# Passes in place of products: the order of the split matmuls within a weight panel, and the halves of a low part at layer doors

## What is computed

```python
# first block (also for a context of 256 tokens, up to w_in)
h = h + 0.5 * g * ((silu(n1(h) @ wg) * (n1(h) @ wu)) @ wd)       # 1024 -> 2816 -> 1024
p = n2(h) @ w_in                                                 # 1024 -> 6144
y = sigmoid(ga) * (o_a @ w_pa) + sigmoid(gb) * (o_b @ w_pb)      # recurrence and long convolution
h = h + m5 * (y @ w_out)
h = h + 0.5 * g * ((silu(n3(h) @ wg) * (n3(h) @ wu)) @ wd)
h = rms_norm(h) * final_norm_w
# second block, twice
proj = rms_norm(h) @ w_in                                        # 1024 -> 7424
h = h + sum(sigmoid(gates) * (branch @ w_branch)) @ w_out        # attention, retention, attention
h = h + relu(rms_norm(h) @ w_mlp_in)**2 @ w_mlp_out              # 1024 -> 4096 -> 1024
```

## Time and profile before

| | us |
|---|---|
| median of 3 runs | 1932.89 |
| lowest, highest | 1930.70, 1933.24 |
| the profiled execution, its own time | 1930.86 |
| its span, first to last instruction | 1929.1 |
| PE busy | 1869.6 (97%) |
| DVE busy | 1269.8 (66%) |
| POOL busy | 590.2 (31%) |
| ACT busy | 356.8 (18%) |

### The profile page before, as it was taken

How to read it: one execution, slowest core, us unless ns; L and a number is a source line. 1 busy time by engine, 2 the same in 40 slices (tenths; PEclk the granted TensorE clock), 3 DMA queues, 4 the chain that set the end, 5 groups by cost and what they waited for, 6 DMA issues and landing times.

```text
span 1929.1 us, 32922 instructions
## 1 busy us (share of the span) xinstructions
PE 1869.6 (97%) x13570; PEld 1712.2 (89%) x13570; DVE 1269.8 (66%) x1424; ACT 356.8 (18%) x655; POOL 590.2 (31%) x745
## 2 busy tenths in 40 slices
PE   4999999998999999999999999999999999999999
PEld 2777777887989979999999998999999999999999
DVE  6663222436268987666687976876667897687666
ACT  3100000103121221211132123321112212432110
POOL 1111111111236313333333222343434332244333
PEclk8999999999999999999999999999999999999999
DMA  9335665331333425354544333444554433344452
GB/s 367 118 109 217 252 245 216 129 109 44 110 132 117 157 88 181 148 179 177 193 154 153 134 131 129 153 175 176 188 181 175 153 132 131 120 162 172 180 180 104
DMA packets 44912, 307.35 MB, mean 159 GB/s; under 512 B 5376, under 2 KB 5888, under 8 KB 8320
## 3 DMA queue, kind: packets, MB, share of 16 engines
q1 hardware_dynamic: 40912, 292.66, 41.4%
q10 hardware_dynamic: 3888, 13.03, 1.9%
HBM read 302.53 MB, written 3.15 MB: 158 GB/s over the span
## 4 chain that ended last, share of the span: by engine, by line
PE 88%; DVE 7%; DMA 1%; issue 1%; ACT 1%; POOL 1%; SPq 0%; DVEq 0%; ACTq 0%; POOLq 0%
PE ps L1898 26%; PE ps L1899 25%; PE ps L1900 25%; PE ps L2030 2%; DMA landing<-in_stream 1%; DVE wlo L681 1%; DVE wlo L683 1%; PE ps L2397 1%; DVE xlo L745 1%; PE ps L2421 1%; PE ps L2407 1%; PE ps L2246 1%; PE ps L2291 1%; PE ps L2370 1%; PE ps L2299 1%
## 5 line engine op out<-in xcount | busy, mean ns | idle before, releaser
L1898 PE MATMUL ps<-xhi,whi 128*128 128x256 f32 (+1 forms) x3680 | 1116.1, 303 | 13.1 <-DVE xlo L691 3.0
L1899 PE MATMUL ps<-xlo,whi 128*128 128x256 f32 (+1 forms) x3680 | 1099.3, 299 | 0.0
L1900 PE MATMUL ps<-xhi,wlo 128*128 128x256 f32 (+1 forms) x3680 | 1098.9, 299 | 0.0
L1898 PEld LDWEIGHTS ps<-xhi,whi 128*128 128x128 f32 x3680 | 705.4, 192 | 50.0 <-issue 18.0
L1899 PEld LDWEIGHTS ps<-xlo,whi 128*128 128x128 f32 x3680 | 705.6, 192 | 22.2 <-issue 1.2
L1900 PEld LDWEIGHTS ps<-xhi,wlo 128*128 128x128 f32 x3680 | 705.2, 192 | 21.0
L681 DVE TENSOR_TENSOR wlo<-landing,whi 128x1024 fp32r<-128x1024 f32 x242 | 428.4, 1770 | 256.5 <-POOL whi L617 255.8
L615 POOL TENSOR_TENSOR whi<-landing,ones 128x16 fp32r<-128x16 f32 x242 | 67.1, 277 | 1321.2 <-PE ps L1900 1281.7
L683 DVE TENSOR_TENSOR wlo<-landing,whi 128x1024 fp32r<-128x1024 f32 x242 | 295.3, 1220 | 0.0
L618 POOL TENSOR_SCALAR whi<-landing 128x1024 fp32r<-128x1024 f32 x242 | 265.0, 1095 | 0.0
L617 POOL TENSOR_SCALAR whi<-landing 128x1008 fp32r<-128x1008 f32 x242 | 261.4, 1080 | 0.1
(11 more groups left out here) (265 smaller groups left out, 1256.7 us busy)
## 6 DMA issues: line engine op xcount, KB each, us to landing
landing<-in_stream SPq DMA_DIRECT2D x250, 1024.0 KB, 4.8
ws<-in_stream SPq DMA_DIRECT2D x28, 1024.0 KB, 5.2
spectra<-big ACTq DMA_DIRECT2D x8, 256.0 KB, 4.3
ws<-spectra ACTq DMA_DIRECT2D x2, 1024.0 KB, 5.1
ws<-in_tabs ACTq DMA_DIRECT2D x1, 1280.0 KB, 5.4
h<-in_xT ACTq DMA_DIRECT2D x1, 1024.0 KB, 6.3
ws<-in_ctxT ACTq DMA_DIRECT2D x1, 1024.0 KB, 15.3
ws<-in_window ACTq DMA_DIRECT2D x1, 1024.0 KB, 13.3
```

Of the source, the lines that this page charges most:

```text
L1898: mm(out, w_hi, x_hi, start=first, stop=False, skip_group_check=True)
L1899: mm(out, w_hi, x_lo, start=False, stop=False, skip_group_check=True)
L1900: return mm(out, w_lo, x_hi, start=False, stop=last, skip_group_check=True)
```

## The change

Each panel's matmuls are put in three passes: all of whi by xhi, all of whi by xlo, all of wlo by xhi, each over k and, within k, over the outputs. The wait for lo_done stands in front of the third pass, and the head of the panel waits for hi_done alone; row panels wait for act_hi at the head and for act_lo in front of the second pass. The last matmul of the second pass counts up a new semaphore, hi_used, and POOL's high part of panel g waits for hi_used of g-2 (and lo_done of g-2) in place of panel_used. Row panels by banks keep the products, with all waits at the head. streamed goes in steps of two k: high by high of one pair, whi by xlo of the pair before, wlo by xhi of the one before that; it waits for norm_hi and norm_lo by pairs and for lo_done in front of its first low matmul. In boundary the first half of the first panel's low part stands behind the first sum, the second half behind all xlo pieces. The context's and the tokens' products of a w_in panel share the three passes; work beside a panel stands behind its second pass.

```diff
@@ POOL
             def high(g, s, turn, n=PANEL):
                 pool.wait_ge(landed[s], (turn + 1) * 16)
                 if not isinstance(g, int) or g >= N_LEAD + 2:
-                    pool.wait_ge(panel_used, g - 1)
+                    pool.wait_ge(hi_used, g - (N_LEAD + 1))
+                    pool.wait_ge(lo_done, g - (N_LEAD + 1))
@@ DVE
+            def low_half(g, s, h2_):
+                c = slice(h2_ * (PANEL // 2), (h2_ + 1) * (PANEL // 2))
+                dve.wait_ge(hi_done, 2 * g - (2 * N_LEAD - 1) + h2_)
+                if h2_ == 0 and (not isinstance(g, int) or g >= N_LEAD + 2):
+                    dve.wait_ge(panel_used, g - 1)
+                ins = v.tensor_tensor(wlo[:, s % 2, c], landing[:, s, c], whi[:, s % 2, c].bitcast(F32), ALU.subtract)
+                if h2_:
+                    ins.then_inc(lo_done, 1)
...
-                residual(out0, end, step_of, next_low)
+                residual(out0, end, step_of, lambda: low_half(g, s, 0))
                 lows(3)
+                low_half(g, s, 1)
@@ PE
+            def highs_in(g):
+                pe.wait_ge(hi_done, 2 * g - 2 * (N_LEAD - 1))
+
+            def lows_in(g):
+                pe.wait_ge(lo_done, g - (N_LEAD - 1))
+
+            def one_pass(w, x, s, job, first=False, last=False, ks=range(KD)):
+                outs, x0, n, token = job
+                for k in ks:
+                    for c, (out, opens) in enumerate(outs):
+                        if token:
+                            a, b = x[:, k, x0 + c * P:x0 + (c + 1) * P], w[:, s % 2, k * COLS:k * COLS + n]
+                        else:
+                            a, b = w[:, s % 2, k * COLS + c * P:k * COLS + (c + 1) * P], x[:, k, x0:x0 + n]
+                        ins = mm(out, a, b, start=first and opens and k == ks[0], stop=last and k == ks[-1],
+                                 skip_group_check=True)
+                return ins
+
+            def panel(g, s, *jobs, beside=None):
+                highs_in(g)
+                for job in jobs:
+                    one_pass(whi, xhi, s, job, first=True)
+                for job in jobs:
+                    last = one_pass(whi, xlo, s, job)
+                last.then_inc(hi_used, 1)
+                if beside is not None:
+                    beside()
+                lows_in(g)
+                for job in jobs:
+                    last = one_pass(wlo, xhi, s, job, last=True)
                 return last
...
+            def row_panel(g, s, row, r, outs, t, first, last):
...
+                highs_in(g)
+                pe.wait_ge(act_hi, row + 1)
+                one(whi, ahi, first, False)
+                pe.wait_ge(act_lo, row + 1)
+                one(whi, alo, False, False).then_inc(hi_used, 1)
+                lows_in(g)
+                return one(wlo, ahi, False, last)
...
-            def streamed(s, outs, x0, t, base, token=False, order=range(KD)):
-
-                for n, k in enumerate(order):
-                    pe.wait_ge(norm_lo, base + (n + 1))
...
-                        last = product(out, *(b + a if token else a + b), n == 0 and opens, n == KD - 1)
+            def streamed(g, s, job, base, order=range(KD), per=1, ends=True):
+                highs_in(g)
+                for n in range(0, KD + 4, 2):
+                    if 4 <= n:
+                        if n == 4:
+                            lows_in(g)
+                        last = one_pass(wlo, xhi, s, job, ks=order[n - 4:n - 2], last=n == KD + 2)
+                    if 2 <= n < KD + 2:
+                        pe.wait_ge(norm_lo, base + per * n)
+                        ins = one_pass(whi, xlo, s, job, ks=order[n - 2:n])
+                        if n == KD and ends:
+                            ins.then_inc(hi_used, 1)
+                    if n < KD:
+                        pe.wait_ge(norm_hi, base + per * (n + 2))
+                        one_pass(whi, xhi, s, job, ks=order[n:n + 2], first=n == 0)
                 return last
...
+            def last_panel(g, s, outs, t, beside=None, behind=None):
+                job, halves = feature(outs, 0, t), (range(KD // 2), range(KD // 2, KD))
+                highs_in(g)
+                one_pass(whi, xhi, s, job, ks=halves[0], first=True)
+                one_pass(whi, xlo, s, job, ks=halves[0])
+                lows_in(g)
+                one_pass(wlo, xhi, s, job, ks=halves[0]).then_inc(x_free, 1)
...
+                one_pass(whi, xhi, s, job, ks=halves[1])
+                one_pass(whi, xlo, s, job, ks=halves[1]).then_inc(hi_used, 1)
...
+                return one_pass(wlo, xhi, s, job, ks=halves[1], last=True)
```

More of the change, by code:

```diff
@@ L1894, in _ @@
             mm = nc.tensor.matmul
[L1896 to L1905, removed]
-                    for k in range(KD):
-                        at_ = k * COLS + c * P
-                        last = product(out, whi[:, s % 2, at_:at_ + P], wlo[:, s % 2, at_:at_ + P], xhi[:, k, x0:x0 + t],
-                                       xlo[:, k, x0:x0 + t], k == 0, k == KD - 1)
-                return last
@@ L1912, in token_panel @@
-            def token_panel(s, outs, x0, n, beside=None):
-                for u, out in enumerate(outs):
-                    for k in range(KD):
-                        x = slice(x0 + u * P, x0 + (u + 1) * P)
-                        c = slice(k * COLS, k * COLS + n)
-                        last = product(out, xhi[:, k, x], xlo[:, k, x], whi[:, s % 2, c], wlo[:, s % 2, c], k == 0, k == KD - 1)
-                    if u == 0 and beside:
-                        beside()
-                return last
@@ L1923, in row_panel @@
-            def row_panel(s, r, outs, t, first, last, by_banks=False, beside=None, order=range(KD)):
+            def highs_in(g):
[13 more added lines that the diff above has]
+                return ins
@@ L1924, in row_panel, with row_panel_by_banks @@
+            def row_panel_by_banks(g, s, row, r, outs, t, first, beside=None, order=range(KD)):
+                highs_in(g)
+                lows_in(g)
+                pe.wait_ge(act_lo, row + 1)
                 for n, j in enumerate(order):
@@ L1982, in one @@
                 def one(i, g, s, begins, ends):
-                    pe.wait_ge(lo_done, g - (N_LEAD - 1))
-                    pe.wait_ge(act_lo, r0 + i + 1)
-                    row_panel(s, r_phase + (s - phase) % UNROLL, outs, t, begins, ends, by_banks and ends,
-                              beside if ends else None, order).then_inc(panel_used, 1)
+                    r = r_phase + (s - phase) % UNROLL
+                    if by_banks and ends:
+                        last = row_panel_by_banks(g, s, r0 + i, r, outs, t, begins, beside, order)
+                    else:
+                        last = row_panel(g, s, r0 + i, r, outs, t, begins, ends)
+                    last.then_inc(panel_used, 1)
                 one(0, g0, phase % UNROLL, True, False)
@@ L2187, in win @@
                 if i >= 6:
-                    last = feature_panel(s, halves_of(bank), 0, T)
+                    last = panel(g, s, feature(opened(halves_of(bank)), 0, T))
                 else:
```

131 lines of the change are left out of this document (61 added, 70 removed).

## The result

The changed kernel takes 1940.92 us (median of 6 runs, 1939.09 to 1941.53) against 1931.59 us of the kernel before (6 runs, 1930.70 to 1933.24): 1.0046 times as long, with a 95% interval of 1.0035 to 1.0057. It is slower by 9.3 us, clear of noise. The forecast was 4.8 us slower, 1937.7 us, so the sign was right and the size too small by half. The 1937.7 looks closer to 1940.92 than the forecast was: it was added to a median of three runs, 1932.89, and the six runs here put the kernel before 1.3 us lower. The two profiled executions, 1930.86 and 1941.53, lie 10.7 us apart; they are compared here.

A forecast was written before the change was run, and what follows sets the result against it. PE, busy 97% of the span, was taken as the bound. Gains of 7.4 us, door losses of 6.8 and clock losses of 5.4 gave +4.8 on 1932.9: 1937.7 us, with an 8-in-10 range of 1929 to 1944.5.

The forecast's parts named there:

- Pace: Dense stretches: the same matmuls in another order, with added waits and increments, cost nothing; upper bound 19 us.
- Rival 4: Waits within a panel keep the next weight load from going ahead; 0.04 us each is +9: 1947 us; chance 0.05.
- What the passes give: Waits at second projection panel, row panels, output projections, DVE's chains and norm doors shrink or go: 7.4 us gained.
- output projections: First two panels of each layer's output projection: waits for low parts go, 1.65 us a layer, 3.3 for two.
- DVE's chains: Waits at 1065.14 and 1096.25 us for DVE work behind a weights' low part: 1.6 us gained for two layers.
- norm door: Stalls at 467.57 and 774.40 us stay; earlier high pieces gain 0.3 us in all, 0.1 at 774.
- The wait at the layer doors: At 963, 1257, 1443, 1735 us PE idles 3.5 us (first 4.2); net loss 1.85 each, first 1.2, 6.8 in all.
- The clock: Half clock after layer-door stalls, 1.7 us at three of four and a little over: 5.4 us lost, bounds 0 and 10.8.
- Rival 1: The clock holds at the layer doors, which stall without loss at 1.2 GHz: 1932.3 us; chance 0.23.
- rival 3: POOL's disturbance hits critical DVE work, 1.6 us not won; half-clock stretches are long, four times 2.7: 1944.7 us; chance 0.15.
- Rival 2: POOL's disturbance falls into DVE's idle time: 2.3 us more at waits, door stalls 1.2 shorter each: 1930.6 us; chance 0.14.
- A rule beside the rows: DVE and POOL lock shared ports, so moving POOL only picks another victim; the 1.6 us becomes nothing or less: 1939.3 us.

The follow-up runs named there:

- experiment 1: The changed kernel with the whole low part of the first panel behind the first sum again at the layer doors: 1927.76 us, ratio 0.9982.
- experiment 3: The changed kernel with PE doing all products with wlo of the layer door's panel last, behind 32 others instead of 12: 1925.40 us, ratio 0.9976.
- experiment 6: The kernel before with only the low part split at the layer doors, second half behind the xlo pieces, products in old order: 1952.35 us, ratio 1.0110.
- experiment 2: The changed kernel with POOL's high part waiting for the whole panel g-2 as before, not for its second pass: 1941.54 us, ratio 1.0056.
- experiment 5: The changed kernel with the whole low part behind the first sum and POOL's high part waiting for the whole panel g-2: 1927.31 us, ratio 0.9970.
- experiment 9: The changed kernel with POOL waiting for the whole panel g-2 and the layer doors' products with wlo last: 1928.01 us, ratio 0.9970.
- experiment 7: The changed kernel with DVE's head scaling one head later and the third output-projection row block's low part before its panel's: 1941.97 us, ratio 1.0056.

## Why the prediction was right in sign, and where its sum fell short

- **Pace.** Right: 13570 matmuls in a new order with waits inside the panels, and the dense pace is the same: in the changed kernel the matmuls of 256 columns that follow another without a wait start 119.5 ns apart on average, as in the kernel before, and from 1280 to 1440 us, over 1333 matmuls, the distance between the two traces stays at 2.57 us. Rival 4 is out.
- **What the passes give.** Right where it rested on single rows: row panels 1.1 for 1.1, output projections 3.2 for 3.3, DVE's chains 1.4 for 1.6 (the wait at 1065 went, the one at 1096 did not). The gains of the table, new stalls left out, are 8.3 for 7.4. That they come out so near is in part luck: the norm door's 1.0 was forecast at 0.1 and is half due to the clock, and the 0.5 in front of 740 was not forecast.
- **The wait at the layer doors.** Right: place, releaser and size. 3.40 to 3.47 us idle at doors two to four for 3.5, 3.83 at the first for 4.2, behind 12 matmuls; 2.1 a door for 1.85. Experiments 1 and 3 show it from DVE's and from PE's side, experiment 6 without the passes. The first door's net loss was worked out as 1.2 because later waits would fall into the delay; they did, 1.0 us came back in front of 986, and the net loss was 2.3 with the clock, 0.9 without.
- **The clock.** Right in kind, low in size: 5.4 in the sum, 7.0 by the table of the doors (6.2 by the medians). The sum took three of four doors and short stretches; it was four of four, one of them long. Rival 1 is out, and so is rival 3's second half, four long ones.
- **Rival 2, DVE relieved more widely.** Out: the wait at 1096 stayed, and at the third door the last four xlo pieces took 2.81 beside POOL, 1.1 more than four of them undisturbed (1.66). The stall has the length that the forecast gave it with that delay in it. The first halves of the low part went from 1770 to 1334 ns, not to the 1.2 us that the prediction names as a sign.
- **The step that failed** is the term for DVE's chains, 1.6. The sentence that goes with it, "the disturbance falls on whatever DVE does two thirds into a panel", only lowered a gain from 3.9 to 1.6; a loss by it was put at nothing in the sum. The gain was nearly right, 1.4. The loss is 5.0 us in two layers; by experiment 2 a POOL that starts late avoids it, but pays 1.2 of it at the last output-projection panels. The victims can be named from the program before: what DVE does when the second pass ends is, at the output projections, the next low part and the row block's low part, on which PE's next pass hangs, and at the last projection the head scaling in front of an eviction. Rival 3's first half names this mechanism, but prices it as the 1.6 not won. With 5.0 more the forecast's +4.8 would have been +9.8, against +9.3 by the medians.
- **A rule beside the rows.** The Trainium skill (SBUF — State Buffer, Who interferes with whom) says that the engine that issues first holds the shared pair for the whole instruction and the other is blocked. The runs agree: 3.96 for 2.36 when POOL came first, undisturbed when DVE did, and then it was POOL's half that took 2.00 for 1.03. By that rule the prediction had the alternative that the move only picks another victim. In DVE's busy time this was not so, 122 us less; in the work that PE waits for it was, and there it cost the 5.0.

Not settled: what sets apart the two groups of runs of experiments 5 and 9. The profiles of upper runs have the stall at 664 and its half-clock stretch, experiment 2's has neither; no profile of a lower run of 5 or 9 was taken.

## What to carry to other kernels

When an operand is made later so that others can be earlier, move its use as well: the same late half cost 3.4 us behind 12 matmuls and 0.2 behind 32. Where an engine is released earlier beside a rival for the same port, look up, stage by stage, what the rival does at that moment and who waits for it; the sum of busy time says nothing on that. And count a stall of PE like these, 3.4 us and more, twice, once for itself and once for the clock behind it; here the second part was 1.5 to 2.6 us a door.

## What the runs showed of the hardware

- Matmuls without use in a wait hold TensorE's clock: with PE busy for 2.9 of the 3.5 us the granted clock stayed at 1.0 (2.4 GHz) at all four doors, without them it was 0.50 (1.2 GHz) at all four. The idle time that remained (0.60 at the second door, 0.97 at the first) did no harm. It is worth 6 us to a kernel that must wait, and it is a way to price the clock apart from the wait.
- The same stall does not always cost the clock. The one at 604 to 605 us (2.16 us idle) is in all twelve profiles; behind it the clock went to 0.50 in eight and stayed full in four (experiments 1, 3, 5 and 9). Experiments 1 and 3 run the same program up to there as the changed kernel, which lost it. Near 698 us PE stands twice, 1.07 and 1.11 us idle, in the kernel before, in the changed one and in experiment 2: at full clock in the first two, with a half-clock stretch in the third. The stalls at the layer doors, 3.4 us and more, cost it each time, in all sixteen cases (the changed kernel, experiments 2, 6 and 7). One profile of a kernel is a sample of this; medians of kernels that differ by a few us need many runs.
- DVE and POOL, reaching their work within half a microsecond of each other, turn a small shift into a large one: 0.8 us of POOL's start went with 1.6 us of DVE, 2.4 us of PE and 6.8 us at half clock (experiments 5 and 2).
